# One of four closing scatter matmuls moved ahead of the wait for the last weights of a decoder layer

## The reference, cut to what matters

```python
for each expert e and the tokens routed to it (top 2 of one group of 8):
    yr = (silu(x_e @ w1[e]) * (x_e @ w3[e])) @ w2[e]      # 1024 -> 512 -> 1024
    out[token] += weight[token, e] * yr
x = x + out
return rms_norm(x, final_norm)                             # mean square over 1024 columns
```

## Time and profile before

| what | value |
|---|---|
| three runs of the kernel | 675.01, 675.29, 675.73 us |
| the profiled execution, span from first to last instruction | 674.2 us |
| its own run time | not given apart from the span; median of the runs less span is 1.1 us |
| TensorE busy | 507.5 us, 75% |
| VectorE, ScalarE, GpSimd busy | 204.2, 145.2, 16.2 us |
| DMA | 244.21 MB, mean 362 GB/s |
| mean granted TensorE clock | 0.885 of full speed |

### The profile page before, as it was taken

How to read it: one execution, slowest core, us unless ns; L and a number is a source line. 1 busy time by engine, 2 the same in 40 slices (tenths; PEclk the granted TensorE clock), 3 DMA queues, 4 the chain that set the end, 5 groups by cost and what they waited for, 6 DMA issues and landing times.

```text
span 674.2 us, 8772 instructions
## 1 busy us (share of the span) xinstructions
PE 507.5 (75%) x3803; PEld 321.7 (48%) x3803; DVE 204.2 (30%) x376; ACT 145.2 (22%) x252; POOL 16.2 (2%) x31
## 2 busy tenths in 40 slices
PE   8999999999999997967644845763474677438475
PEld 7999998999999742412311411231141123114121
DVE  4798665588857431100000100000010000001002
ACT  5764545354545511000000000000000000000002
POOL 1200010001001000000000000000000000000001
PEclk9999999999999988997956988796697778579889
DMA  9899433608899999999999999999999999999993
GB/s 292 257 333 371 173 125 125 250 1 307 301 387 385 417 372 431 428 428 428 429 427 428 427 429 428 428 428 427 430 427 430 424 431 426 430 425 430 424 409 146
DMA packets 49113, 244.21 MB, mean 362 GB/s; under 512 B 9064, under 2 KB 18736, under 8 KB 37296
## 3 DMA queue, kind: packets, MB, share of 16 engines
q1 hardware_dynamic: 49072, 243.62, 89.4%
HBM read 242.53 MB, written 4.22 MB: 366 GB/s over the span
## 4 chain that ended last, share of the span: by engine, by line
PE 52%; DMA 43%; SPq 2%; DVE 1%; ACT 1%; issue 1%; POOL 0%; POOLq 0%
PE ps L711 16%; DMA slots_late<-in_w 13%; PE ps L1073 11%; DMA slots_own<-in_w 9%; DMA attn_data<-in_w 7%; PE ps L734 7%; PE ps L1078 6%; DMA slot_last<-in_w 4%; DMA slot_mixed<-in_w 4%; DMA slot_spare<-in_w 3%; SPq L544 1%; PE ps L689 1%; DMA slots_own<-in_w_in 1%; PE ps L833 1%; PE ps L862 1%; PE ps L1183 1%
## 5 line engine op out<-in xcount | busy, mean ns | idle before, releaser
L1073 PE MATMUL ps<-slots_late,x_sb 128*32 128x512 f32 x320 | 86.3, 689 | 39.3 <-DMA slots_late<-in_w 16.2
L1073 PE MATMUL ps<-slot_spare,x_sb 128*32 128x512 f32 x128 | 59.4, 663 | 14.3 <-DMA attn_data<-in_w 14.3
L1810 DVE TENSOR_TENSOR slot_extra<-ps,slot_extra 128x512 f32<-128x512 f32 x8 | 5.5, 692 | 212.2 <-ACT slot_extra L1437 212.2
L1073 PE MATMUL ps<-attn_data,x_sb 128*32 128x512 f32 x160 | 61.3, 698 | 10.7 <-DMA slots_own<-in_w 10.7
L435 DVE TENSOR_TENSOR w_low<-slots_own,w_high 128x2048 fp32r<-128x2048 f32 (+1 forms) x32 | 64.7, 2022 | 15.2 <-ACT w_high L1247 14.9
L1434 ACT ACTIVATE slot_extra<-ps 128x256 f32<-128x256 f32 x8 | 3.1, 384 | 299.9 <-PE ps L1141 299.9
L1078 PE MATMUL ps<-slots_own,slot_extra 128*32 128x512 f32 x192 | 49.5, 719 | 16.5 <-DMA slots_late<-in_w 8.8
L1073 PE MATMUL ps<-slots_own,x_sb 128*32 128x512 f32 x240 | 53.3, 630 | 9.3 <-DMA slot_last<-in_w 3.4
L1078 PE MATMUL ps<-attn_data,slot_extra 128*32 128x512 f32 x112 | 46.3, 746 | 16.7 <-DMA slots_own<-in_w 16.7
L1247 ACT ACTIVATE w_high<-slots_own 128x2048 fp32r<-128x2048 f32 (+1 forms) x32 | 54.2, 1696 | 20.2 <-PE ps L734 10.8
L711 PE MATMUL ps<-h_high,w_high 128*128 128x256 f32 x224 | 55.4, 288 | 0.0
(11 more groups left out here) (258 smaller groups left out, 866.8 us busy)
## 6 DMA issues: line engine op xcount, KB each, us to landing
slots_own<-in_w SPq DMA_DIRECT2D x27, 2048.0 KB, 33.4
slots_late<-in_w SPq DMA_DIRECT2D x23, 2048.0 KB, 34.8
attn_data<-in_w SPq DMA_DIRECT2D x16, 2048.0 KB, 33.9
slot_last<-in_w SPq DMA_DIRECT2D x9, 2048.0 KB, 36.4
slots_own<-in_w_in SPq DMA_DIRECT2D x8, 2048.0 KB, 12.4
slot_spare<-in_w SPq DMA_DIRECT2D x8, 2048.0 KB, 35.6
slot_mixed<-in_w SPq DMA_DIRECT2D x7, 2048.0 KB, 35.5
slots_own<-in_w_out SPq DMA_DIRECT2D x2, 2048.0 KB, 8.7
```

The costliest lines, as they stand in the source:

```text
L1073: return pe.matmul(ps[SLOTS * e:SLOTS * e + SLOTS, 4 + matrix, :], xeT[:, k, SLOTS * e:SLOTS * e + SLOTS], w, start=(k == 0), stop=(k == K ...
L1810: dve.tensor_tensor(act_sb, ps[:, 5, :].rearrange("p (q f) -> p f q", f=FC), silu_sb.rearrange("p (f q) -> p f q", f=FC), ALU.mult).then_i ...
```

## The change

In the last expert step, TensorE now waits for selwT_copied and y_copied_a and issues the scatter matmul (0, 0) between column half 0 and the wait for last_half_in. The loop at the end of the step leaves this matmul out. The three semaphore signals keep their order. No operation is added or removed in number, and no other engine's code is changed.

```diff
+                def scatter(c, t):
+                    return pe.matmul(ps[:, 2 * t + c, :], selwT[:, t * P:(t + 1) * P], y_sb[:, 512 * c:512 * c + 512],
+                                     start=False, stop=True, skip_group_check=True)
...
                     for c in range(2):
                         if c:
+                            pe.wait_ge(selwT_copied, it + 2)
+                            pe.wait_ge(y_copied_a, it + 2)
+                            scatter(0, 0).then_inc(summed, 1)
                             pe.wait_ge(last_half_in, 16)
                         for e in range(SHARE):
                             m = down_matmul(c, 3, e, w[:, e, 512 * c:512 * c + 512])
...
                 for c in range(2):
                     pe.wait_ge((y_copied_a, y_copied_v)[c], it + 2)
                     for t in range(TT):
-                        m = pe.matmul(ps[:, 2 * t + c, :], selwT[:, t * P:(t + 1) * P], y_sb[:, 512 * c:512 * c + 512],
-                                      start=False, stop=True, skip_group_check=True)
-                        if slices_out and c + t < 2:
+                        if slices_out and c + t == 0:
+                            continue
+                        m = scatter(c, t)
+                        if slices_out and c + t == 1:
                             m.then_inc(summed, 1)
                 m.then_inc(added, 1)
```

## The result

| | runs | median | range |
|---|---|---|---|
| kernel before | 5 | 675.29 us | 675.01 to 675.81 us |
| changed kernel | 5 | 677.54 us | 677.00 to 678.75 us |

What follows compares the result with a forecast made beforehand. TensorE's row of scatter records was taken to set the pace at the end. 0.86 us saved less 0.18 us delay gave 0.68 us, so 675.29 us becomes 674.6 us, range 673.7 to 675.9 us.

Steps and rivals of the forecast that it cites:

- The price of the matmul: Scatter row at the end: one matmul, two records at 0.43 us each, leaves it, taking off 0.86 us.
- When it starts: Moved matmul starts 0.06 us after ScalarE's copy, at 662.25 us, its first record taking 0.43 us.
- the delay of column half 1: After the inserted matmul, column half 1 starts at 663.20 us in place of 663.02 us, 0.18 us late.
- The switch back: TensorE's return from the full array to 32-column tiles ahead of column half 1 costs 0.09 us.
- The other copy: VectorE's copy of column half 1 is hidden by matmul (0, 1) with 0.08 us to spare.
- Rival A: Between column halves: gap closes, matmul delays column half 1; no gain at 1.88 us, up to 1.0 us lost; chance 0.07.
- g: Time from TensorE's start on column half 0 to the landing of the last half; read as 2.56 us.
- Rival C: Last half lands 2.74 us or more after column half 0 starts: insertion free, 0.86 us gained, 674.4 us; chance 0.09.
- Behind it nothing is in the way.: After the last scatter record, squares, sum, rstd, last product and output all move along with the 0.68 us gain.
- rival B: Matmul hidden without gain, another limit right behind; at the low clock 675.5 us; chance 0.08.
- Rival D: Shift not due to the scatter, from DMA stream rate or moved code; beyond 0.2% either way; chance 0.06.

Runs made afterwards that it cites:

- e13_before_norounds: Kernel before without TensorE's closing branch and its code for further rounds, which this input does not enter; median 675.42 us.
- e9_before_fsq: Kernel before, with TensorE waiting for the first square (fsq) ahead of its closing branch; median 676.60 us, ratio 1.0016.
- e14_after_norounds: Changed kernel without TensorE's closing branch and its code for further rounds, which this input does not enter; median 675.03 us.
- e1_null: Kernel before with four blank source lines and nothing else; median 675.64 us, ratio 1.0004.
- e2_waits: Kernel before plus the two added waits ahead of the wait for the last half, no matmul moved; median 675.66 us, ratio 1.0005.
- e4_count: Kernel before plus two long-satisfied waits behind the last scatter matmul of the last step; median 674.99 us, ratio 0.9992.
- e12_before: Kernel before, unchanged, run once more; median 675.50 us, ratio 0.9990.
- e6_after_hold: Changed kernel, with TensorE held ahead of its closing branch until SyncE has issued the four outputs; median 677.61 us, ratio 1.0029.

## Why the prediction was wrong, step by step

**The price of the matmul: right.** 0.86 us taken off the row; measured 0.83 us from column half 1 to the first output issue, in all four traces of the changed program.

**When it starts, and the delay of column half 1: too small.** From column half 0 to column half 1 it takes 2.88 to 2.90 us where 2.74 us was worked out. ScalarE released TensorE in 0.14 us (662.68 + 0.60 to 663.42), not in the 0.06 us taken from a release by VectorE, and the first record held the array 0.50 us, not 0.43 us. Where the weights release column half 0, column half 1 is 0.38 us late, not 0.18 us. The switch back cost 0.09 us as worked out. The Trainium skill, TensorEngine Tiling (Array Packing), section Key Properties, puts a drain there; the trace again shows less: the tiled record starts at 664.44 us, 0.07 us before the last full-array record ends.

**The other copy: right.** TensorE waited for VectorE's copy and lost 0.03 us by it, 3.27 us from column half 1 to the last record where 3.24 us follows from 4.10 - 0.86.

**Rival A: right in form, wrong in chance.** Its point of decision is 2.04 us with the measured terms (2.90 - 0.86), not 1.88 us. Four of eight traces with a moved matmul lie below it: g was 1.72, 1.84, 1.86 and 0.12 us. I gave 0.07. I had read a 0.22 us idle time ahead of column half 0 as slack in TensorE's favour. It is the margin between two chains of nearly equal length, and one of them depends on when the clock rises in the last step: at 645.8 us in the trace I read, at 647.1 to 648.4 us in seven others. What separates the traces is how long the up product of the last step (L1073 before) had run by then: 5.0 to 6.0 us in these four and in e13_before_norounds, 2.8 to 4.1 us in the eleven others, where g is 2.39 to 2.54 us. Rival C's g of 2.74 us or more came in none. In the trace of before g is 2.51 us, to the landing at 662.97 us; the 2.56 us of the prediction runs to the start of column half 1.

**The failing step: "Behind it nothing is in the way."** I named the output as moving along and did not ask what else runs beside it. TensorE's last fetch starts 6.04 to 6.43 us behind column half 1 in the traces of kernels with the old order and no added hold, 6.13 to 6.90 us in those of the changed program: it moved with every wait that was added ahead of the closing branch, and without one it hangs, I infer, on the last wait that TensorE passes, the one for the right copy, which the change leaves in place. The first output issue hangs on the last scatter, and that moved from 6.34 to 5.51 us. Before, the fetch began with or ahead of the output and held only its second issue, which the transfer of the first partly covers: 4.1 to 4.6 us to the last landing. Now it begins 0.6 to 1.4 us into the output, and it takes 5.4 to 5.7 us. The means are 4.31 us (five traces) and 5.54 us (four): **1.23 us lost against 0.83 us gained**, and 0.3 to 1.1 us more by the delay of column half 1. That makes 0.7 to 1.5 us from one trace of each run, and the 0.8 us of all runs lies at its lower end. From the landing to the end the changed kernel took 11.6 us (664.06 to 675.70), where 10.5 us was drawn and the kernel before took 11.2 us. e9_before_fsq shows that a later fetch costs as much with no matmul moved, though in another way, e13_before_norounds and e14_after_norounds that without it the saving is there.

The trace of before had it all: the long second issue and the packet in q8. The Trainium skill, Runtime: NRT & Kernel Launch, section Instruction fetch mechanics, says that instructions come in blocks of 16 KiB over a DMA queue of the sequencer and that a taken branch beyond the loaded window forces a fetch. The traces agree: 32 such packets, and the last two move with TensorE's branch and go with it.

**The clock** was at its higher level, 2.4 GHz, from column half 0 to the scatter in all traces with the change, so the low clock of rival B did not come. **Rival D** was real: the landing of the last half moved by 2.4 us over the sixteen traces (661.77 to 664.13 us), in both orders. The +1.09 us ahead of the moved matmul lies within that. But the four traces of the changed program have the landing at 663.02 to 664.13 us and the five of the old one at 662.18 to 663.44 us, so it is not shown that none of it comes with the change.

What stays open: by what means a packet of instructions holds an issue, why the issue ends 0.2 to 0.5 us behind the end of the packet, and whether the fetch could be had earlier without leaving code out, which was not tried.

## What to carry to other kernels

Work moved off the end shifts everything behind it against everything that is pinned to another event; list both, instruction fetches of every engine among them, before calling the rest of the chain free. When the transfer at the end takes only a few microseconds, look in the traces for fetches beside it, and keep branches with large bodies away from there. A gap in one trace is a margin between two chains: price the insertion at the smallest gap that other executions show.

## What the runs showed of the hardware that I had not expected

One late 16 KB instruction fetch is a single packet of 0.93 to 1.45 us. In each of the eleven traces where it overlaps the output issues it held exactly one of them, which took 0.6 to 1.8 us in place of 0.37 to 0.46 us and ended 0.2 to 0.5 us behind it. Overlap alone was not enough: in four traces (e1_null, e2_waits, e4_count, e12_before) the first output issue lay wholly inside the packet and took 0.37 us, and the second was held. With the issues done, the last output packets still came up to 1.6 us late (e9_before_fsq, 5.70 us against 4.1 us).

The first rise of the granted clock came 3.9 to 6.6 us behind the first instruction in sixteen traces, the first rise in the last step at 645.6 to 648.4 us. In each of the sixteen the one in the last step lies 641.7 us behind the first of all, so an execution that begins with a late rise has a late one here too. TensorE reached column half 0 between 0.04 and 3.01 us behind its weights. The two latest, 2.45 and 3.01 us, are the two traces in which the clock fell once more within the last step (e6_after_hold, e13_before_norounds).
